# Splitting ScalarE's part of the quarters' join, and the order of join, bonus sums and state steps, in an RWKV and two-layer S5 block

## The reference, cut to what matters

```python
def step(S, inp):
    r_t, w_t, k_t, v_t, a_t, b_t = inp
    sa = jnp.einsum('bhij,bhj->bhi', S, a_t)
    S = S * w_t[:, :, None, :] + sa[..., None] * b_t[:, :, None, :] + v_t[..., None] * k_t[:, :, None, :]
    y = jnp.einsum('bhij,bhj->bhi', S, r_t) if emit else None
    return S, y
...
bonus = jnp.sum(r * (k_dir[0] + k_dir[1]) * r_k, -1, keepdims=True) * v
```

```python
dt = jnp.exp(log_dt.astype(jnp.float32))[:, None]
a_bar = jnp.exp(lam * dt)
b_bar = ((a_bar - 1.0) / lam)[..., None] * b_mat
```

## Time and profile before

| what | value |
|---|---|
| median of 3 runs | 1208.63 us (1206.26 to 1215.55) |
| the profiled execution: own time | 1215.1 us |
| the profiled execution: span, first to last instruction | 1213.3 us |
| TensorE busy | 1143.9 us (94%) |
| TensorE weight loads busy | 796.1 us (66%) |
| VectorE busy | 641.5 us (53%) |
| ScalarE busy | 338.0 us (28%) |
| GpSimd busy | 112.8 us (9%) |
| mean granted TensorE clock | 0.96 of full |

### The profile page before, as it was taken

How to read it: one execution, slowest core, us unless ns; L and a number is a source line. 1 busy time by engine, 2 the same in 40 slices (tenths; PEclk the granted TensorE clock), 3 DMA queues, 4 the chain that set the end, 5 groups by cost and what they waited for, 6 DMA issues and landing times.

```text
span 1213.3 us, 15588 instructions
## 1 busy us (share of the span) xinstructions
PE 1143.9 (94%) x6191; PEld 796.1 (66%) x6191; DVE 641.5 (53%) x1350; ACT 338.0 (28%) x788; POOL 112.8 (9%) x107
## 2 busy tenths in 40 slices
PE   5899999979788898999999999999999999999998
PEld 2444857657778586546568888744556478888543
DVE  3222115757897944699515665640698226656400
ACT  2212223755553222424221112200525121221100
POOL 0000101210120011054000000010161000000000
PEclk9799999988788986999999999999999999999999
DMA  9722332000003202453237454323532264444410
GB/s 356 261 70 83 113 139 75 1 1 1 2 1 99 96 12 70 143 204 139 70 96 225 143 172 170 139 105 109 203 139 70 70 199 148 139 139 166 177 38 35
DMA packets 96665, 140.05 MB, mean 115 GB/s; under 512 B 12207, under 2 KB 63058, under 8 KB 96466
## 3 DMA queue, kind: packets, MB, share of 16 engines
q1 hardware_dynamic: 96228, 138.94, 33.6%
q10 hardware_dynamic: 366, 0.13, 0.0%
HBM read 138.01 MB, written 1.05 MB: 115 GB/s over the span
## 4 chain that ended last, share of the span: by engine, by line
PE 74%; DVE 19%; ACT 2%; DMA 2%; issue 2%; POOL 0%; SPq 0%; DVEq 0%; ACTq 0%
PE bank L1334 25%; PE bank L1353 12%; PE bank L825 11%; PE bank L480 2%; PE bank L473 2%; DMA ring<-in_ada_w 2%; PE bank L1162 2%; DVE work L2584 1%; PE bank L1096 1%; PE bank L619 1%; PE bank L1152 1%; DVE work L2579 1%; PE bank L1045 1%; DVE ring L2152 1%; DVE rot L2564 1%
## 5 line engine op out<-in xcount | busy, mean ns | idle before, releaser
L1334 PE MATMUL bank<-work,ring 128*128 128x256 f32 x1024 | 222.7, 379 | 0.0
L1334 PEld LDWEIGHTS bank<-work,ring 128*128 128x128 f32 x1024 | 194.2, 190 | 26.2
L825 PE MATMUL bank<-work,ring 128*128 128x256 f32 (+1 forms) x432 | 141.0, 485 | 2.4 <-ACT work L1404 2.4
L1353 PE MATMUL bank<-ring,work 128*128 128x512 f32 x288 | 124.2, 592 | 0.0
L825 PEld LDWEIGHTS bank<-work,ring 128*128 128x128 f32 x432 | 82.7, 194 | 56.0 <-issue 49.4
L1857 ACT ACTIVATE work<-work,prm 128x256 f32<-128x256 f32 x88 | 48.0, 593 | 250.5 <-DVE work L2724 224.0
L1353 PEld LDWEIGHTS bank<-ring,work 128*128 128x128 f32 x288 | 54.7, 190 | 68.0 <-issue 67.4
L2716 DVE TENSOR_TENSOR work<-bank,turned 128x512 f32<-128x512 f32 x44 | 30.4, 692 | 112.0 <-PE bank L1334 111.9
L1334 PE MATMUL bank<-work 128*128 128x256 f32 x384 | 83.9, 379 | 0.0
L1334 PEld LDWEIGHTS bank<-work 128*128 128x128 f32 x384 | 73.0, 190 | 9.9
L2734 DVE SCALAR_TENSOR_TENSOR work<-work,prm 128x256 f32<-128x256 f32 x176 | 77.1, 480 | 4.2 <-ACT work L1857 2.6
(11 more groups left out here) (453 smaller groups left out, 1758.9 us busy)
## 6 DMA issues: line engine op xcount, KB each, us to landing
ring<-in_w_up SPq DMA_DIRECT2D x32, 1024.0 KB, 7.7
ring<-in_w_in SPq DMA_DIRECT2D x24, 1024.0 KB, 7.5
ring<-in_w_down SPq DMA_DIRECT2D x16, 1024.0 KB, 6.1
ring<-in_ada_w SPq DMA_DIRECT2D x12, 1024.0 KB, 11.1
work<-in_w_up SPq DMA_DIRECT2D x12, 1024.0 KB, 8.2
ring<-in_w_out SPq DMA_DIRECT2D x10, 1024.0 KB, 6.2
work<-in_w_in SPq DMA_DIRECT2D x4, 1024.0 KB, 8.5
work<-in_w_down SPq DMA_DIRECT2D x4, 1024.0 KB, 6.1
```

Source lines behind the costliest of these rows:

```text
L825: ins = mm(b[0:rows, 0:toks], wt[:, k, off:off + rows], hT[:, k, 0:toks], start=(k == 0), stop=(k == KD - 1))
L1334: ins = mm(b[:, SEQ * half:SEQ * half + SEQ], wt[:, KD * half + k, P * j:P * j + P], xnT[:, k, :], start=(k == 0), stop=(k == KD - 1))
L1353: ins = mm(acc[2 * t + j][:, :], actT[:, k, P * t:P * t + P], wt[:, q, 512 * j:512 * j + 512], start=(k == 0), stop=(k == FB - 1))
```

## The change

It has four edits, in three queues:
1. VectorE: the first of the two transposes signals a semaphore of its own, `row_inv`, in place of the step counter, and VectorE does not wait for it before the second transpose.
2. ScalarE: `spread_quarters` makes the two diagonal copies of direction 0 (from `by_row`, after `row_inv`), then copies the middle products, then makes the two diagonal copies of direction 1 (from `by_column`, after `t_inv`).
3. TensorE: in the second join the bonus sums come after the corners.
4. VectorE: `join(1)` comes before `state_steps(0)`.

```diff
@@ TensorE, join_quarters @@
                 ins.then_inc(*filling(("mid", p)))
-                if p:
-                    bonus_sums()
                 pe.wait_ge(*when_empty(("mid", p)))
                 pe.wait_ge(*turn(("corner", p)))
...
                 ins.then_inc(*filling(("corner", p)))
+                if p:
+                    bonus_sums()
@@ ScalarE @@
             def spread_quarters(p):
 
-                act.wait_ge(S["t_inv"], p + 1)
-                for d in range(2):
+                def diagonals(d):
+                    act.wait_ge(S[("row_inv", "t_inv")[d]], p + 1)
                     for q in range(2):
                         ins = A.activation(of_direction(t64[:, :, 32 * q:32 * q + 32], d), of_direction((by_row, by_column)[d], d), ACT.Copy, scale=C("quad_par", 2)[:, q:q + 1])
                     ins.then_inc(S["t64_diag"], 1)
+                diagonals(0)
                 key = ("mid", p)
                 act.wait_ge(*when_full(key))
                 if p:
                     act.wait_ge(*when_empty(("st", 3)))
                 b = bank_of(key)
                 A.activation(mid, b[:, :], ACT.Copy).then_inc(*emptying(key))
+                diagonals(1)
@@ VectorE, the end of invert @@
-                step(V.transpose(sq_c.rearrange("p (n x) -> p x n", n=32), t3))
+                V.transpose(sq_c.rearrange("p (n x) -> p x n", n=32), t3).then_inc(S["row_inv"], 1)
+                aside(next(passed))
                 V.transpose(sq_d.rearrange("p (n y) -> p y n", n=32), t3.transpose([0, 2, 1])).then_inc(S["t_inv"], 1)
@@ VectorE, the main order @@
             ins.then_inc(S["bonus_in"], 1)
+            join(1)
             state_steps(0)
-            join(1)
             state_inputs(0)
```

More of the change, by code:

```diff
@@ L173 @@
  lam_exp lam_sum lora lw_in k_rate maps_used m_bias mix_gmlp mix_rw mix_ssm mod_cols off_made off_step out_done p2_load pads
- params_1 params_2 q_tok qk_rot qk_rstd qk_sum qk_taken qk_turned qk_var r_ch r_grown rk_used rotated rotated_used rstd_1 rstd_f rstd_lat scale_a scanned
+ params_1 params_2 q_tok qk_rot qk_rstd qk_sum qk_taken qk_turned qk_var r_ch r_grown rk_used rotated rotated_used rstd_1 rstd_f rstd_lat scale_a scanned row_inv
  sine ssq ssq_a ssq_f t64_diag turns_abs t_inv tables u_theta us var_1 var_a var_f vec_step vg_n vg_rstd vg_var weights_used
```

## The result

The changed kernel takes 1218.42 us (median of 10 runs, 1215.17 to 1220.64). Runs of the kernel before, taken beside it, have a median of 1213.45 us (10 runs, 1205.32 to 1215.55). The ratio is 1.0059 with a 95% interval of 1.0037 to 1.0081. So the change makes the kernel slower by 7 us, between 4.5 and 9.8 us; the two medians lie 5.0 us apart. That is inside the 1% which the prediction took for about what a measurement can tell from no change, but this measurement's interval excludes no change. The forecast was +3.2 us.

What follows compares the result with a forecast made beforehand. VectorE's small work ahead of add_cross was taken to bound the second join: +3.15 state steps, +1.80 ScalarE parameters, +0.08 lost overlap, -1.22 earlier join, -0.64 shorter remainder. That +3.2 on 1208.6 gave 1211.8 us, range 1205.0 to 1218.5.

Steps and rivals of the forecast that it cites:

- edit 2: Second join: with two diagonal copies ahead instead of four, the corners start 1.22 us earlier and the join ends at 421.10.
- the series of edit 4: Behind the second join: state steps 3.15 us, ScalarE's parameters, state inputs 3.05 us and bonus product delay add_cross by 3.17 us.
- The price of the bank: Before add_cross: the first group of "cross" waits for the bank that the first bonus product frees, costing 0.6 us.
- the table load: ScalarE between exponential and sine: 1.28 us and no more; by the skill's drain rule 1.4 us longer.
- TensorE ... needs 1.09 us for 16 matmuls: First group of "cross" before add_cross: its 16 matmuls take 1.09 us as before, so add_cross starts at 431.03.
- old rhythm: From add_cross on: VectorE's eight additions and TensorE's "last" follow as before, so all 3.2 us reach the end.
- rival A: TensorE's clock falls in the new 3.9 us gap behind the first solves, costing 4 us more: 1215.8; chance 0.25.
- the sum in absolute terms carries over: Whole kernel: the +3.2 us from the profiled execution is added to the median 1208.6, giving 1211.8.
- edit 1 and the first join: Transposes' signal and earlier first-join corners: 0 us each, bounds -0.1 and 0 for the signal, -0.2 and 0 for the join.
- B: Second join: its 1.22 us lead reaches the end because VectorE's small work does not hold add_cross: 1207.4; chance 0.12.
- C: First join: earlier corners keep TensorE's clock at full, its transposes 1.2 us shorter and as much behind: 1209.4; chance 0.06.
- D: Second join: the middle products' copy gains nothing, the join stays at 422.3, only exposed work counts: 1213.0; chance 0.07.

Runs made afterwards that it cites:

- e2: The changed kernel with join(1) put back behind state_steps(0); ratio to the kernel before 1.0000.
- e4: The kernel before with only join(1) moved ahead of state_steps(0); ratio to the kernel before 1.0058.
- e8: The changed kernel with both bonus products directly behind the join, ahead of the state steps; ratio to the kernel before 1.0016.
- e5: The changed kernel with the fourth group of the first solves computed four times over, filling TensorE's gap; ratio to the kernel before 1.0004.
- after_3: Third profile of the changed kernel, nothing altered; span 1215.7 us, of which early projection's end to propagation's start 23.9 us.
- e3: The changed kernel with the bonus sums put back ahead of the corners; ratio to the kernel before 1.0087.
- before_2: Second profile of the kernel before, nothing altered; span 1206.3 us, of which early projection's end to propagation's start 19.0 us.
- before_3: Third profile of the kernel before, nothing altered; span 1212.1 us, of which early projection's end to propagation's start 18.7 us.
- after_2: Second profile of the changed kernel, nothing altered; span 1213.9 us, of which early projection's end to propagation's start 23.8 us.
- e7: The changed kernel with halved bonus sums and all state work behind the solves, the join directly behind the bonus inputs; ratio to the kernel before 1.0007.
- e1: The kernel before with only the transposes' signal and the split of ScalarE's copies changed; ratio to the kernel before 0.9983.
- e6: The changed kernel with the join behind the state steps, bonus sums halved around the corners, bonus products ahead of state_inputs; ratio to the kernel before 0.9984.

## Why the prediction was right or wrong

**Right: what bounds.** The chain behind the join did stay on VectorE's small work, and the loss sits where it was put. e2 and e4 show that edit 4 carries it all.

**Right: edit 2.** Corners at 2.50 us after the early projection; forecast 2.48.

**Right, with a remainder: the series of edit 4.** State steps 3.1 us, ScalarE's part with a wait of 1.79 us for VectorE (forecast 1.80), state inputs 3.07 us. "Cross" begins at 14.34 after the early projection; forecast 14.06. The 0.28 us are a pause of 0.18 us inside the corners and a run to the join that was 0.2 us longer besides, less 0.1 us by which the state steps overlapped the join. The price of the bank, forecast at 0.6 us, also came out (e8 against e5).

**Right: the table load.** It cost 1.28 us on the path, and the sine followed at once. The drain that the Trainium skill adds (ScalarE: Activation LUTs, What ACT_TABLE_LOAD costs) did not show in this row either, now that the load is on the critical chain.

**Wrong: "TensorE ... needs 1.09 us for 16 matmuls", the last term of the sum, and the "old rhythm" behind it.** That is the step that failed. The gap of 4.24 us in front of it dropped the clock, the first group took 2.01 us, and the additions stretched from 5.63 to 6.2 us. S grew by 5.0 us instead of 3.2. Of these, 3.5 belong to the exposed work (the 3.2 and the 0.3 of the corners) and 1.5 to the clock (0.9 in the first group, 0.6 in the rhythm); e5 against after_3 gives 1.3 for the clock. It was also one of the prediction's own signs of being wrong: a clock below full between 426 and 447. I had this as rival A, with a chance of 0.25 and a time of 1215.8, and had weighed it too low: one row in which the clock survived some 2 us of idleness in 4 stood against one in which it fell with 3.2 us idle, and the new gap was nearer to the second. The rule of the Trainium skill on idle gaps (TensorE: Matmul & The Clock Gate, Why this matters for your kernels) spoke for the fall, and all three executions bear it out. e3, e4 and before_2 show besides that the clock can fall where TensorE has idled for no more than 1.51 us at a time. Rival A was the mechanism, on top of the forecast's. But its price in S was 1.5 us, where I had taken 4 between two bounds. That its total, +7.2 us, is so near the measured +7 is luck.

**Wrong: "the sum in absolute terms carries over" to the median.** The median of the three runs shown was 1208.6, on the low side: all 77 timed executions of the kernel before run from 1205.3 to 1215.8 with a median of 1213.5; 19 are below 1210 and 43 above 1213. Beside the changed kernel the kernel before had 1213.45. So of the 6.6 us by which 1218.4 is above the forecast of 1211.8, 4.8 are the base and 1.8 are S. That 1218.4 still lies just inside the range, below 1218.5, is no merit of the sum. Whether the change costs more than the 5.0 us of S stays open: the interval (4.5 to 9.8 us) includes 5.0. For more speaks that the lowest of 12 executions of the changed kernel is 1215.2, which is 1210.2 with S's 5.0 taken off, and over a quarter of those of the kernel before are below that.

**Right in four executions of six: edit 1 and the first join.** From the end of VectorE's second transpose to TensorE's transposes for the next case, before_3 has 313.35 to 323.78 and after_2 312.57 to 322.97, 10.4 us both; the first profile of the kernel before and after_3 have 10.4 too:

```profile
311.23 2.12 DVE L2164 STREAM_TRANSPOSE ring<-ring 128x1024 f32<-128x1024 f32 x1
...
323.78 2.82 PE L609 MATMUL bank<-con,work 128*128 128x128 f32 x12 [1.76 <-DVE work L2027]
```

```profile
310.49 2.08 DVE L2167 STREAM_TRANSPOSE ring<-ring 128x1024 f32<-128x1024 f32 x1
...
322.97 2.82 PE L609 MATMUL bank<-con,work 128*128 128x128 f32 x12 [2.64 <-DVE work L2029]
```

In the two others (before_2 and the first profile of the changed kernel) TensorE began the middle products over 4 us after the transposes. From there on the changed kernel took 9.3 us against 8.8. Its corners started 1.2 us earlier and then paused, which gave the lead away and more:

```profile
320.53 0.25 PE L707 MATMUL bank<-ring,work 32*32 32x32 f32 x4 [1.54 <-issue]
```

That is 0.5 us outside the bounds of the forecast (-0.2 and 0), in one execution.

**Rivals B, C and D.** B (the lead reaches the end) and D (no lead) fell: the lead was there and was swallowed. C had no effect to see: the matmuls behind the first join (L609) took 2.82 us in all three executions of the changed kernel, as in two of the kernel before.

## What to carry to other kernels

Small work that fills a wait is free only as long as it stands in the wait; moved behind the awaited step, it goes onto the path with everything on other engines that hangs on it, here 3 us on VectorE and 1.8 on ScalarE for a lead of 1.2. Put later still, it is free only if nothing waits there either (e7). When a change opens a gap on TensorE of about the length of one beside which the trace already shows a fall of the clock, put the lower clock into the sum, not into a rival. And where executions differ by more than the change, compare a stretch between two fixed instructions over several profiles before reading the totals.

## What the runs showed of the hardware that was not expected

- The three repetitions of 16 matmuls in e5, useless as work, kept the clock and took the ratio from 1.0059 to 1.0004.
- When the corners start earlier, TensorE pauses among them for nothing that the profile names ("issue"). In the 128 corners there is no pause at a start of 3.7 us after the early projection (four executions), none in e1 and 0.28 us in e3 at a start of 3.1, and at a start of 2.5 between 0.18 and 0.96 us: 0.18, 0.26 and 0.56 in the three executions of the changed kernel, 0.62 in e6, 0.77 in e2, 0.96 in e7. So of the split's lead of 1.2 us a part is lost there, a different part each time. The cause was not tested.
- The executions of one kernel spread over 10 us, and the same 16 matmuls at about 500 us take 3.69 or 5.36 us in two of them, depending on the granted clock.
- The clock fell with TensorE idle for no more than 1.51 us at a time (before_2, and the first falls in e3 and e4); in the two other profiles of the kernel before, with the same idle times, it did not.
